# FFN loops of a DiT block pair: 512 + 256 token columns re-tiled as 384 + 384

## The reference

```python
def swiglu(x, w_in, w_out):
    a, b = jnp.split(x @ w_in, 2, axis=-1)
    return (jax.nn.silu(a) * b) @ w_out

h = h + 0.5 * mod_l[:, 2] * swiglu(pre_norm(h, norm_g[i, 0], mod_l, 0), ffn_w_in[i, 0], ffn_w_out[i, 0])
g = g + 0.5 * mod_c[:, 2] * swiglu(pre_norm(g, norm_g[i, 0], mod_c, 0), ffn_w_in[i, 0], ffn_w_out[i, 0])
```

## Time and profile before

| | |
|---|---|
| median of 3 runs | 3221.36 us (3219.93 to 3228.47) |
| the profiled execution | 3219.45 us, its span 3217.5 us |
| PE busy | 3081.1 us (96%), 17592 matmuls |
| DVE busy | 1821.1 us (57%) |
| ACT busy | 870.2 us (27%) |
| chain that ended last | PE 90%, DVE 6%, ACT 2%, issue 1% |

### The profile page before, as it was taken

How to read it: one execution, slowest core, us unless ns; L and a number is a source line. 1 busy time by engine, 2 the same in 40 slices (tenths; PEclk the granted TensorE clock), 3 DMA queues, 4 the chain that set the end, 5 groups by cost and what they waited for, 6 DMA issues and landing times.

```text
span 3217.5 us, 42601 instructions
## 1 busy us (share of the span) xinstructions
PE 3081.1 (96%) x17592; PEld 2642.6 (82%) x17592; DVE 1821.1 (57%) x2652; ACT 870.2 (27%) x1192; POOL 36.8 (1%) x73
## 2 busy tenths in 40 slices
PE   6999999879999999999999999999899999999999
PEld 4888888757777788888888888888788888888887
DVE  4675565735654577555566455656745546465444
ACT  3211111333443442111114111111322223242221
POOL 0000000000000000000000000000000000000000
PEclk8999999989999999999999999999899999999999
DMA  6333222110101033333231123323112111122222
GB/s 239 131 131 104 104 104 93 57 40 27 52 26 52 27 118 131 109 113 104 91 117 53 66 104 104 104 91 104 53 47 72 66 52 66 53 79 92 92 95 87
DMA packets 40977, 277.72 MB, mean 86 GB/s; under 512 B 4352, under 2 KB 5632, under 8 KB 8000
## 3 DMA queue, kind: packets, MB, share of 16 engines
q1 hardware_dynamic: 31024, 205.85, 18.1%
q0 software_dynamic: 9872, 70.72, 6.3%
HBM read 274.45 MB, written 2.10 MB: 86 GB/s over the span
## 4 chain that ended last, share of the span: by engine, by line
PE 90%; DVE 6%; ACT 2%; issue 1%; DMA 0%; SPq 0%; DVEq 0%; ACTq 0%
PE ps L300 29%; PE ps L301 28%; PE ps L302 28%; PE ps L614 2%; PE ps L328 1%; DVE wl L1237 1%; DVE act_buf L1321 1%; ACT wh L869 1%; DVE xnl L1325 1%; PE ps L314 1%; DMA ada_w<-ada 0%; DVE nrm L1534 0%; ACT xnh L900 0%; PE ps L346 0%; PE ps L413 0%
## 5 line engine op out<-in xcount | busy, mean ns | idle before, releaser
L300 PE MATMUL ps<-xnh,wl 128*128 128x512 f32 (+1 forms) x3040 | 1063.2, 350 | 32.3 <-DVE wl L1237 14.7
L301 PE MATMUL ps<-xnl,wh 128*128 128x512 f32 (+1 forms) x3040 | 1052.0, 346 | 0.0
L302 PE MATMUL ps<-xnh,wh 128*128 128x512 f32 (+1 forms) x3040 | 1051.7, 346 | 0.0
L300 PEld LDWEIGHTS ps<-xnh,wl 128*128 128x128 f32 x3040 | 581.1, 191 | 115.5 <-DVE xnl L1325 16.6
L302 PEld LDWEIGHTS ps<-xnh,wh 128*128 128x128 f32 x3040 | 580.6, 191 | 70.8
L301 PEld LDWEIGHTS ps<-xnl,wh 128*128 128x128 f32 x3040 | 581.3, 191 | 68.5 <-issue 1.0
L1237 DVE TENSOR_TENSOR wl<-raw,wh 128x2048 fp32r<-128x2048 f32 (+1 forms) x183 | 410.2, 2241 | 141.6 <-ACT wh L869 141.4
L869 ACT ACTIVATE wh<-raw 128x2048 fp32r<-128x2048 f32 (+1 forms) x178 | 332.8, 1871 | 578.2 <-PE ps L302 578.2
L1379 DVE SCALAR_TENSOR_TENSOR h<-ps,coef,h 128x512 f32<-128x512 f32 x624 | 371.7, 642 | 116.1 <-PE ps L302 115.5
L300 PE MATMUL ps<-hidh,wl 128*128 128x512 f32 (+1 forms) x1232 | 425.0, 345 | 3.1 <-DVE h L1337 3.1
L301 PE MATMUL ps<-hidl,wh 128*128 128x512 f32 (+1 forms) x1232 | 426.0, 346 | 0.0
(11 more groups left out here) (226 smaller groups left out, 3069.3 us busy)
## 6 DMA issues: line engine op xcount, KB each, us to landing
raw<-weights SPq DMA_DIRECT2D x183, 1024.0 KB, 4.9
adaw<-ada POOLq DMA_DIRECT2D x64, 1024.0 KB, 5.1
ada_w<-ada SPq DMA_DIRECT2D x8, 1024.0 KB, 20.5
h<-x_in SPq DMA_DIRECT2D x1, 2048.0 KB, 9.0
c_act<-c_rows POOLq DMA_DIRECT2D x2, 1024.0 KB, 5.1
out<-h SPq DMA_DIRECT2D x8, 256.0 KB, 2.0
h<-x_in SPq DMA_DIRECT2D x1, 1024.0 KB, 29.0
cs<-rope_mla POOLq DMA_DIRECT2D x1, 512.0 KB, 3.4
```

The costliest lines, as they stand in the source:

```text
L300: mm(dst, lhs[1][rows], rhs[0][rows], start=first, stop=False)
L301: mm(dst, lhs[0][rows], rhs[1][rows], start=False, stop=False)
L302: return mm(dst, lhs[0][rows], rhs[0][rows], start=False, stop=last)
```

## The change

In the loops the 768 columns of both streams are cut in two equal groups of 384 (`GROUPS`); the boundary now lies inside the latent tokens. `up(j)` uses four banks, 4j to 4j+3: `a` of both groups, then `b` of both. `down` uses four sets of two banks, 2(m mod 4) and the next. ACT and DVE read 2 x 384 columns from two banks in one instruction each, where they had one for 512 and one for 256. `add_y` has three pieces, 384 + 128 + 256, since the coefficient differs between streams. The FFN with 512 tokens alone keeps one group of 512 with banks 4j and 4j+2, and 0, 2, 4, 6 in `down`. What stands in front of the loops and behind them keeps its tiles and banks.

PE's looped `up(0)` waits for two counts of `hid_done` at once. `down` waits for them at m = 0 and m = 2, and for adds from m = 4 on, four pieces back. Behind `down` PE waits for 6 of the 8 adds, and `up(1)` waits for all 8.

```diff
-Y_SETS = ((6, 7), (0, 2), (3, 5))
+R_BANKS = (6, 0, 3)
+HALF_T = T // 2
+GROUPS = ((0, HALF_T), (HALF_T, HALF_T))
...
             def ffn(n_streams, slot, parts=STREAMS, start=False):
-                streams = STREAMS[:n_streams]
+                groups = GROUPS if n_streams == 2 else STREAMS[:1]
...
-                def up(j, s, y_left=None):
-
-                    pe.wait_ge(w_ready[s], c.next(w_ready[s]))
-                    pe.wait_ge(hid_done, c.next(hid_done))
-                    groups = [(1, 3 * j + 1, 0, STREAMS[0]), (0, 3 * j, 0, STREAMS[0])] + \
-                        [(0, 3 * j + 2, 0, STREAMS[1]), (1, 3 * j + 2, L, STREAMS[1])] * (n_streams - 1)
-                    for g, (half, bank, col, part) in enumerate(groups):
-                        if g == 1 and y_left is not None:
-                            pe.wait_ge(y_added, c.next(y_added, y_left))
-                        ins = chain(half, s, bank, col, part)
+                def up(j, s):
+
+                    for half in range(2):
+                        for i, part in enumerate(groups):
+                            ins = chain(half, s, 4 * j + 2 * half + i, 0, part)
                     ins.then_inc(glu_full, 1)
...
                     for m in range(KD):
-                        if m in (1, 2):
-                            pe.wait_ge(hid_done, c.ahead(hid_done, m))
-                        if m >= 3:
+                        if m in (0, 2):
+                            pe.wait_ge(hid_done, c.ahead(hid_done, 1 + m // 2))
+                        if m >= 4:
                             pe.wait_ge(y_added, c.next(y_added))
-                        for i, (t0, n) in enumerate(streams):
+                        for i, (t0, n) in enumerate(groups):
                             for kk in range(2):
-                                ins = three(ps[:, Y_SETS[m % 3][i], 0:n], w(s, kk * D + m * P),
+                                ins = three(ps[:, 2 * (m % 4) + i, 0:n], w(s, kk * D + m * P),
...
-                    up(0, s0, y_left=0)
-                    up(1, s1)
-                    down(0, s0)
-                    up(0, s1, y_left=3)
-                    up(1, s0)
-                    down(1, s1)
-                    c.next(y_added, 3)
+                    for par in range(2):
+                        sa, sb = (s0, s1) if par == 0 else (s1, s0)
+                        pe.wait_ge(w_ready[sa], c.next(w_ready[sa]))
+                        pe.wait_ge(hid_done, c.next(hid_done, 2))
+                        up(0, sa)
+                        pe.wait_ge(w_ready[sb], c.next(w_ready[sb]))
+                        pe.wait_ge(y_added, c.next(y_added, 2 * par))
+                        up(1, sb)
+                        down(par, sa)
+                        pe.wait_ge(y_added, c.next(y_added, 2))
+                    c.next(y_added, 2)
...
+                        if n_streams == 2:
+                            ins = fn(act_buf[:, j, :].rearrange("p (i t) -> p i t", i=2), ps[:, 4 * j:4 * j + 2, 0:HALF_T], ACT.Silu)
+                        else:
+                            ins = fn(act_buf[:, j, 0:S], ps[:, 4 * j, :], ACT.Silu)
...
-                for i, (t0, n) in enumerate(STREAMS[:n_streams]):
-                    bank = Y_SETS[n_y % 3][i]
-                    ins = stt(out=h[:, m, t0:t0 + n], in0=ps[:, bank, 0:n], scalar=coef[:, 1, m, i:i + 1],
+                if n_streams == 2:
+                    b = 2 * (m % 4)
+                    parts = ((b, 0, 0, HALF_T), (b + 1, 0, HALF_T, S - HALF_T), (b + 1, S - HALF_T, S, L))
+                else:
+                    parts = ((2 * (m % 4) if n_y is None else R_BANKS[n_y % 3], 0, 0, S),)
+                for bank, col, t0, n in parts:
+                    j = int(t0 == S)
+                    ins = stt(out=h[:, m, t0:t0 + n], in0=ps[:, bank, col:col + n], scalar=coef[:, 1, m, j:j + 1],
                               in1=h[:, m, t0:t0 + n], op0=ALU.mult, op1=ALU.add)
```

More of the change, by code:

```diff
@@ L352, in last_y @@
                 for m in range(KD):
-                    if m == 2:
-                        pe.wait_ge(y_added, c.ahead(y_added, 0))
+                    if m in (1, 2):
+                        pe.wait_ge(y_added, c.ahead(y_added, m - 2))
                     if m >= 3:
@@ L515, in ffn @@
                     for m in range(KD):
-                        if m < 2:
-                            pe.wait_ge(y_added, c.ahead(y_added, m - 1))
-                        if m >= 3:
+                        if m in (2, 3):
+                            pe.wait_ge(y_added, c.ahead(y_added, m - 3))
+                        if m >= 4:
                             pe.wait_ge(y_added, c.next(y_added))
-                        y(m, STREAMS[0], Y_SETS[m % 3][0], 0).then_inc(y_full, 1)
+                        y(m, STREAMS[0], 2 * (m % 4), 0).then_inc(y_full, 1)
                 return 1 - slot
@@ L848, in head @@
                             pe.wait_ge(y_added, c.next(y_added))
-                        y(n_y % KD, STREAMS[0], Y_SETS[n_y % 3][0], 0).then_inc(y_full, 1)
+                        y(n_y % KD, STREAMS[0], R_BANKS[n_y % 3], 0).then_inc(y_full, 1)
                 if not last:
@@ L938, in up @@
                     act.wait_ge(glu_full, c.next(glu_full))
-                    a, a_at = FIRST_CTX[j][0:2] if first else (3 * j + 2, 0)
                     if first:
                         split_hi(s)
+                        ins = fn(act_buf[:, j, 0:S], ps[:, 3 * j, :], ACT.Silu)
+                        if n_streams == 2:
+                            a, a_at = FIRST_CTX[j][0:2]
+                            ins = fn(act_buf[:, j, S:T], ps[:, a, a_at:a_at + L], ACT.Silu)
                     else:
                         act.wait_ge(hid_ready, c.next(hid_ready))
-                    ins = fn(act_buf[:, j, 0:S], ps[:, 3 * j, :], ACT.Silu)
-                    if n_streams == 2:
-                        ins = fn(act_buf[:, j, S:T], ps[:, a, a_at:a_at + L], ACT.Silu)
+                        if n_streams == 2:
+                            ins = fn(act_buf[:, j, :].rearrange("p (i t) -> p i t", i=2), ps[:, 4 * j:4 * j + 2, 0:HALF_T], ACT.Silu)
+                        else:
+                            ins = fn(act_buf[:, j, 0:S], ps[:, 4 * j, :], ACT.Silu)
                     ins.then_inc(silu_done, 1)
@@ L1373, in add_y @@
             def add_y(m, n_streams, n_y=None):
-                n_y = m if n_y is None else n_y
                 dve.wait_ge(y_full, c.next(y_full))
-                for i, (t0, n) in enumerate(STREAMS[:n_streams]):
-                    bank = Y_SETS[n_y % 3][i]
-                    ins = stt(out=h[:, m, t0:t0 + n], in0=ps[:, bank, 0:n], scalar=coef[:, 1, m, i:i + 1],
+                if n_streams == 2:
+                    b = 2 * (m % 4)
[5 more added lines that the diff above has]
+                    ins = stt(out=h[:, m, t0:t0 + n], in0=ps[:, bank, col:col + n], scalar=coef[:, 1, m, j:j + 1],
                               in1=h[:, m, t0:t0 + n], op0=ALU.mult, op1=ALU.add)
@@ L1388, in up @@
                         split_lo(s)
-                    b, b_at = FIRST_CTX[j][2:4] if first else (3 * j + 2, L)
                     dve.wait_ge(silu_done, c.next(silu_done))
-                    ins = tt(act_buf[:, j, 0:S], act_buf[:, j, 0:S], ps[:, 3 * j + 1, :], ALU.mult)
-                    if n_streams == 2:
-                        ins = tt(act_buf[:, j, S:T], act_buf[:, j, S:T], ps[:, b, b_at:b_at + L], ALU.mult)
+                    if first:
+                        ins = tt(act_buf[:, j, 0:S], act_buf[:, j, 0:S], ps[:, 3 * j + 1, :], ALU.mult)
+                        if n_streams == 2:
+                            b, b_at = FIRST_CTX[j][2:4]
+                            ins = tt(act_buf[:, j, S:T], act_buf[:, j, S:T], ps[:, b, b_at:b_at + L], ALU.mult)
+                    elif n_streams == 2:
+                        both = act_buf[:, j, :].rearrange("p (i t) -> p i t", i=2)
+                        ins = tt(both, both, ps[:, 4 * j + 2:4 * j + 4, 0:HALF_T], ALU.mult)
+                    else:
+                        ins = tt(act_buf[:, j, 0:S], act_buf[:, j, 0:S], ps[:, 4 * j + 2, :], ALU.mult)
                     ins.then_inc(hid_done, 1)
```

## The result

The changed kernel takes 3264.26 us (median of 4 runs, 3262.95 to 3266.11), the kernel before 3220.74 us beside it (4 runs, 3219.93 to 3228.47). The ratio is 1.013, interval 1.0116 to 1.0144: slower by 1.3%. The profiled execution took 3265.37 us with a span of 3263.7, so the span grew by 46.2 us.

What follows compares the result with a forecast made beforehand. The prediction took PE, busy 96% of the span, to bound the kernel: 3219.45 + 41.5 (entry) + 7.0 (clock) - 1.5 (matmuls) = 3266.5 us, range 3250 to 3290.

Steps and rivals of the forecast that it cites:

- The entry, 41.5 us: PE's first looped matmul of each FFN waits for unit 1's gating: 15.15, 15.16, 5.55, 5.04 us plus restarts.
- Why the wait stands there: At the looped up(0): bank 3 still holds unit 1's half, so its first matmul waits for two counts of hid_done.
- The clock behind the stalls, 7.0 us: PE behind the four entry stalls: lower granted clock loses 1.75 us each; bounds 0 and 12 us.
- Matmuls in the ups, 0.1733: Looped ups: 384 columns cost 0.1733 us on the straight line, two of them 0.3467, nothing gained.
- Matmuls in the downs, between 0.1733 and 0.1760: Looped downs: middle of these spacings, block 50.05 against 50.10 us, -1.5 us over 30 blocks.
- Adds on DVE, 0: Third add piece costs 0.12 us per output piece; heaviest down's sixth add ends 0.8 us in time, cost 0.
- DVE's busy time: Sign on the profile page: DVE busy up by about 40 us from 1821.
- FFN 4, 0: Loop of the 512-token FFN: same matmuls in other banks, 0 us.
- Rival (a): All 8640 looped matmuls: 384 columns cheaper than the line; at 0.162 us 98 us saved, 3170 us; chance 0.05.
- (b): Loop entries: the wait costs nothing, unit 0 releases PE's first looped matmul all the same; 3218 us; chance 0.03.
- (c): Looped matmuls: entry as forecast, 384 columns at 0.1760 us everywhere; 3286 us; chance 0.06.
- (d): Heavy downs: DVE's third add piece makes PE wait, 4 stalls, 3267 to 3270 us; forecast with it 0.86.

Runs made afterwards that it cites:

- Experiment 1: Changed kernel with the first block's unit 1 moved out of the looped up(0)'s banks, up(0) waiting for one count: 3215.92 us, ratio 0.9977.
- experiment 2: Kernel before, old tiles and banks, with only the looped up(0) taking both counts: 3269.26 us, ratio 1.0141.
- experiment 3: Changed kernel with DVE's modulation work of the first block moved behind unit 1's gating, two-count wait kept: 3249.66 us, ratio 1.0078.
- experiment 4: As experiment 3, with ACT's activation of the conditioning rows also moved behind unit 1: 3245.68 us (one run).
- Experiment 5: Experiment 1 with downs and adds back to 512 + 256 columns, ups kept at 384 + 384: 3219.06 us, ratio 0.9986.
- experiment 6: Experiment 1 with each of the three add pieces cut in two, six adds per output piece: 3226.14 us, ratio 1.0011.
- experiment 9: Experiment 1 with a bank of its own for each of FFN 4's 8 output pieces, down having 2 waits instead of 6: 3215.18 us, ratio 0.9977.
- experiment 10: Experiment 9 with two output pieces of FFN 4's downs interleaved, the bank changing every 3 matmuls instead of 6: 3223.85 us (one run).

## Why the prediction was right

Forecast 3266.5 us, measured 3264.26; for the profiled execution 3265.37. The direction and the mechanism held; the steps in turn:

- **The entry, 41.5 us: right.** Measured 41.3 (15.20, 15.44, 5.59 and 5.08 more than the 0.12 of before). Experiment 1 takes the wait away and gets all of it back; experiment 2 puts it alone into the old tiles and pays all of it. What made this term exact was that DVE's queue in front of the loop waits for nothing that the change touches, so the end of unit 1's gating could be read from the trace of before.
- **Why the wait stands there: wrong in part.** I wrote that bank 3 makes the first matmul wait. The first matmul writes bank 0. Bank 3 is written first by the fourth chain, 72 matmuls or 12.5 us later, and in FFN 4 not at all (`up(0)` has banks 0 and 2 there). By the code, ACT's silu of unit 1 is what reads bank 3. In FFN 1 it was done long before:

```profile
91.09 0.58 ACT L942 ACTIVATE act_buf<-ps 128x512 f32<-128x512 f32 x1
```

  That is 91.67. Without the stall PE's `up(0)` would have started at 102.30 - 15.20 = 87.10 and come to bank 3 at 99.6. So in time the bank was free, and the loss comes from taking both counts in front of the first chain. With the second count in front of the fourth chain I estimate a stall of 15.2 - 12.5 = 2.7 us in FFN 1, about 3 in FFN 2 and none in FFN 3 and 4; no run tried that.
- **The clock behind the stalls, 7.0 us: right in size.** The first pairs of ups grew by 7.6 us at a granted clock of 0.50 for 3 to 6 us; in experiment 2 by 9.0. The loss did not grow with the stall: stalls of 15 us cost 1.6 to 1.8 us, those of 5 us 1.4 and 2.8. The even 1.75 us per stall was no property of them: in experiments 2, 3 and 4 the four stalls together cost 9.0, 9.6 and 9.2 us, so 7.0 lay at the low end.
- **Matmuls in the ups, 0.1733: right.** From 1320.31 to 1353.59, 192 matmuls of 384 columns took 33.28 us, 0.1733 each:

```profile
1320.31 0.34 PE L302 MATMUL ps<-xnh,wl 128*128 128x384 f32 x1
...
1353.59 0.33 PE L302 MATMUL ps<-hidh,wl 128*128 128x384 f32 x1
```

- **Matmuls in the downs, between 0.1733 and 0.1760: mis-sized.** This is the step that failed, in its size. I carried the slower spacing of 512-column downs over to 384 columns in proportion to the columns. Measured, 96 matmuls from 1303.67 to 1320.31 took 16.64 us, 0.1733 each, on the line. The block is 49.93 and not 50.05, and over 30 of them the change gains 30 x 0.17 = 5.1 us instead of 1.5. Experiment 5 shows that this gain is the downs'.
- **Adds on DVE, 0: right,** and 1.1 us in time where 0.8 was forecast. What I wrote on DVE's busy time was wrong: it rose by 25 us, not about 40. The groups by shape of the changed kernel (count, busy us, mean ns, idle before) answer to the earlier trace rows:

```profile
L1388 DVE SCALAR_TENSOR_TENSOR h<-ps,coef,h 128x384 f32<-128x384 f32 x240 | 147.0, 612 | 57.5 <-PE ps L304 55.4
L1388 DVE SCALAR_TENSOR_TENSOR h<-ps,coef,h 128x256 f32<-128x256 f32 x240 | 113.8, 474 | 0.0
L1388 DVE SCALAR_TENSOR_TENSOR h<-ps,coef,h 128x128 f32<-128x128 f32 x240 | 81.9, 341 | 0.0
```

  The three means sum to 1.427 us, against 0.747 + 0.474 = 1.221 before. But instructions in a row overlap by some 0.08 us and the page counts that once, so 240 third pieces add 240 x 0.12 = 29, and 60 merged gatings take back about 4. The line on the path used 0.12; the forecast of the page's sum used 0.20.
- **FFN 4, 0: right,** 297.00 us for nine blocks in both kernels.
- **Rival (a)**, 384 columns cheaper than the line: fell, the spacing is 0.1733 in both places. The Trainium skill ("TensorE: Matmul & The Clock Gate", section "Back-to-back issue gap") has N / 2.4 + 2.5 ns, by which 384 columns take 162.5 ns as an estimate, and calls that the gap of an isolated matmul, not of a stream with weight loads; no long run here shows less than 173 ns for 384 columns. The price of (a), 98 us, was a mix: it set the 0.162 us of the Trainium skill's formula against a measured pair of 0.3467. By that formula alone 384 + 384 and 512 + 256 both take 325.0 ns, and the change would gain nothing. My argument against (a) was weak too: a line through two widths has the same fixed part at both by construction. What settles it is the third width. **(b)** fell with the four waits, and experiments 1 and 2 show that the counts are what matters. **(c)** fell: 384 columns have a mean of 0.1733 in ups and downs, not 0.1760. **(d)** stayed inside the forecast, and experiment 6 shows its point of decision to be real.

The profiled executions add up by the segments: 3219.45 + 41.3 + 7.6 - 4.7 + 2.0 = 3265.65, and 0.3 us less lie outside the span, which gives 3265.4 (measured 3265.37). Beside that the forecast had 3.2 us too little gain by the tiles, 0.2 too much for the entry, 0.6 too little for the clock, and nothing for the 2.0 of the stretches between or the 0.3 outside the span: -3.2 - 0.2 + 0.6 + 2.0 - 0.3 = -1.1 us. That it came within 1.1 us is luck in part, since these cancel.

## What to carry to other kernels

When tiles are laid out anew over banks, look first at the loop's entry: which bank of the first looped step is still held by what stands in front of the loop, which matmul writes it first, and when its reader ends by the trace of before. Here one wait, put in front of the first chain for a bank that the fourth one writes, cost 49 us in four places, in a change whose tiles gain 5. Moving two banks in front of the loop and taking the counts one at a time makes it faster than both kernels. Where a wait takes several counts at once, price it by the last of them, and when the work in front of it is moved, look at the queue of each engine in the chain, not only at the one named as releaser.

## What the runs showed of the hardware

- The spacing of fp32 matmuls with a weight load each is on one straight line for 256, 320, 384 and 512 columns in the ups (0.1200, 0.1467, 0.1733, 0.2267 us), and 448 columns are off it by 3 to 6 ns (0.2027 to 0.206). In the downs, with chains of 6, 512 columns take 0.233 (FFN 4), while 384 stay at 0.1733. Neither fewer waits nor other turns of the banks changed the 0.233 (experiments 9 and 10).
- At the lower clock level (granted clock 0.50) steps behind the first entry were 0.32 us apart for 384 columns, which is 384 / 1.2 = 320 ns with nothing on top; at the upper level the measured 173.3 ns are 13 more than 384 / 2.4 = 160:

```profile
103.11 0.52 PE L304 MATMUL ps<-xnh,wh 128*128 128x384 f32 x1
103.43 0.52 PE L302 MATMUL ps<-xnh,wl 128*128 128x384 f32 x1
```

- What PE loses in clock behind a stall does not follow the length of the stall here: in the changed kernel idle times of 15 us cost 1.6 and 1.8 us, those of 5 to 6 us 1.4 and 2.8.
